# Where attention ends and the Fourier part begins in the branch stretch of the second block's two layers

## What is computed

```python
for l in range(DEPTH_2):                      # 2
    ...
    ux = hx @ w_in[l]
    uc = hc @ (w_in[l] if ctx_out else w_in[l][:, OFF_K:OFF_HQ])
    fx = fourier_mix(col(ux, OFF_FOURIER, FOURIER_W), w_four[l])
    ax, ac = attention_group(ux, uc, base_c, q_norm[l], k_norm[l], tabs, ctx_out)
    rx, rc = hgrn_group(ux, uc, base_c, lb_all[:, l], hg_norm[l], ctx_out)
    x = x + g_a * (jnp.concatenate([fx, ax, rx], axis=-1) @ w_out[l])
    x = x + g_f * swiglu(rmsnorm_2(x) * (1 + sc_f) + sh_f, w_gate[l], w_up[l], w_down[l])
    ...

def fourier_mix(u, w):                        # 4 groups of 64 features
    z = u.astype(jnp.float32).reshape(b, n, FOURIER_GROUPS, FOURIER_GD)
    z = jnp.fft.fftn(z, axes=(1, 3), norm="ortho").real
    return z.reshape(b, n, FOURIER_W).astype(u.dtype) @ w
```

## Time and profile before

| what | us |
| --- | --- |
| median of 3 runs | 2682.14 |
| lowest and highest of them | 2682.07 and 2695.03 |
| the profiled execution | 2682.28 |
| its span in the profile | 2680.5 |
| PE busy | 2499.0 (93%) |
| DVE, ACT, POOL busy | 874.3, 795.4, 784.0 |

### The profile page before, as it was taken

The page is one execution under the profiler, slowest core; times in us unless marked ns, Lnnn a source line. Parts: engine busy times, 40 slices in busy tenths (PEclk is TensorE's granted clock), DMA queues, the critical chain, the costliest instruction groups (busy, mean ns, idle before and its releaser), DMA issues.

```text
span 2680.5 us, 38133 instructions
## 1 busy us (share of the span) xinstructions
PE 2499.0 (93%) x16690; PEld 1926.0 (72%) x16690; DVE 874.3 (33%) x1301; ACT 795.4 (30%) x1016; POOL 784.0 (29%) x262
## 2 busy tenths in 40 slices
PE   7997888999999999979899999999799878899998
PEld 5884566777777786446788888888578336788886
DVE  3003236255257433832511111112451642311113
ACT  4222233223234423423322122122432433322222
POOL 2232143333333222502222222222221412344442
PEclk9997899999999999979999999999899878999999
DMA  4431023444443101002111111111211002222221
GB/s 171 166 140 32 17 95 142 172 157 157 157 169 139 57 9 46 3 2 95 48 63 63 63 63 59 68 41 62 73 40 46 2 2 95 79 95 95 104 93 55
DMA packets 41574, 216.70 MB, mean 81 GB/s; under 512 B 4088, under 2 KB 13064, under 8 KB 18112
## 3 DMA queue, kind: packets, MB, share of 16 engines
q1 hardware_dynamic: 37032, 206.55, 21.0%
q10 hardware_dynamic: 4376, 7.71, 0.9%
HBM read 212.12 MB, written 2.13 MB: 80 GB/s over the span
## 4 chain that ended last, share of the span: by engine, by line
PE 76%; DVE 7%; ACT 3%; issue 1%; POOL 0%; DMA 0%; DVEq 0%; ACTq 0%; POOLq 0%
PE PS L667 60%; PE PS L670 3%; PE PS L1087 2%; DVE s_states L1486 2%; PE PS L1120 2%; PE PS L744 1%; DVE a_lo L590 1%; PE PS L1683 1%; PE PS L1787 1%; DVE tmp L597 1%; PE PS L1882 1%; PE PS L1137 1%; PE PS L1099 1%; DVE x L610 1%; PE PS L728 0%
## 5 line engine op out<-in xcount | busy, mean ns | idle before, releaser
L2012 POOL TENSOR_TENSOR w_lo<-raw,w_hi 128x2048 fp32r<-128x2048 f32 (+2 forms) x146 | 650.8, 4457 | 1560.6 <-ACT w_hi L780 1560.6
L667 PE MATMUL PS<-a_hi,w_hi 128*128 128x512 f32 (+1 forms) x2104 | 702.4, 376 | 56.8 <-DVE a_lo L590 30.3
L667 PE MATMUL PS<-a_lo,w_hi 128*128 128x512 f32 (+1 forms) x2104 | 687.3, 369 | 0.0
L667 PE MATMUL PS<-a_hi,w_lo 128*128 128x512 f32 (+1 forms) x2104 | 681.9, 366 | 0.0
L667 PEld LDWEIGHTS PS<-a_hi,w_hi 128*128 128x128 f32 x2104 | 364.0, 191 | 154.6 <-issue 76.3
L667 PEld LDWEIGHTS PS<-a_hi,w_lo 128*128 128x128 f32 x2104 | 365.8, 192 | 68.9
L667 PEld LDWEIGHTS PS<-a_lo,w_hi 128*128 128x128 f32 x2104 | 365.3, 192 | 62.1 <-issue 0.7
L780 ACT ACTIVATE w_hi<-raw 128x2048 fp32r<-128x2048 f32 (+2 forms) x146 | 270.4, 1852 | 339.8 <-PE PS L667 185.1
L667 PE MATMUL PS<-hid_hi,w_hi 128*128 128x512 f32 (+1 forms) x784 | 260.5, 369 | 2.8 <-issue 2.8
L667 PE MATMUL PS<-hid_lo,w_hi 128*128 128x512 f32 (+1 forms) x784 | 260.9, 369 | 0.0
L667 PE MATMUL PS<-hid_hi,w_lo 128*128 128x512 f32 (+1 forms) x784 | 258.5, 366 | 0.0
(11 more groups left out here) (220 smaller groups left out, 2479.8 us busy)
## 6 DMA issues: line engine op xcount, KB each, us to landing
raw<-in_w_ada SPq DMA_DIRECT2D x48, 1024.0 KB, 6.9
raw<-in_w_ff SPq DMA_DIRECT2D x32, 1024.0 KB, 4.8
raw<-in_w_in SPq DMA_DIRECT2D x27, 1024.0 KB, 4.8
raw<-in_w_gate SPq DMA_DIRECT2D x22, 1024.0 KB, 4.8
raw<-in_w_up SPq DMA_DIRECT2D x22, 1024.0 KB, 4.8
raw<-in_w_down SPq DMA_DIRECT2D x16, 1024.0 KB, 4.7
raw<-in_w_out SPq DMA_DIRECT2D x12, 1024.0 KB, 5.5
raw<-in_w_down SPq DMA_DIRECT2D x8, 768.0 KB, 4.2
```

Of the source, the lines that this page charges most:

```text
L667: mm = p.matmul(ps[:, dst], wv[:, k, idx * P:(idx + 1) * P], av[:, k, dst], start=first, stop=last)
L2012: pool.tensor_tensor(w_lo[:, m % 2, 0:kt, 0:ncol], src, w_hi[:, m % 2, 0:kt, 0:ncol].bitcast(F32), ALU.subtract).then_inc(s_lo.sem, 1)
```

## The change

One constant. It is read by `att_pos`, through `other_pe`, `other_act` and `other_dve`, and by `four_pos`, so it moves attention and the Fourier part against the scan on PE, ACT and DVE, in both layers of the second block.

```diff
--- before.py
+++ after.py
@@ -1746,7 +1746,7 @@
                 except StopIteration:
                     left.remove(head)
 
-        ATT_SHARE = 0.8
+        ATT_SHARE = 0.7
         GATED_SHARE = 0.8
 
         def other_pe(p, l):
```

## The result

The changed kernel took 2715.07 us (median of four runs, 2708.99 to 2718.67), the kernel before 2683.72 beside it: 31 us or 1.2% between the medians, and a measured ratio of 1.0098, with an interval of 1.0079 to 1.0118. The forecast was 2676 with a range to 2688. The kernel became slower, by more than any of my cases gave.

What follows compares the result with a forecast made beforehand. TensorE, busy 93% of the span, was taken as the bound, with gains only in its idle or low-clock stretches. Layer 0's -2.9 and layer 1's -3.3 gave -6.2 us from 2682.28, so 2676.1; range 2667 to 2688.

Steps and rivals of the forecast that it cites:

- Covered edits: Readout and w_out panel behind the last outputs, VectorE's inverses: reordering there costs nothing; bounds 1.5 and 2 us.
- rival 4: The panel of w_out or an inverse is late by its bound: 2679 us, chance 0.1.
- Behind the last outputs: Feature tiles leave the stretch before the out projection: minus 4.5 us in layer 0, minus 5.0 in layer 1.
- From the third outputs' end to the last updates: Attention leaves this stretch, two tiles enter: minus 6.1 us in layer 0, minus 5.9 in layer 1.
- The last chain of states: VectorE's states before the last outputs: attention's product comes earlier, minus 0.4 us (layer 0) and 0.6 (layer 1); outputs still low-clocked.
- The same attention, earlier: Attention moved ahead hardly falls into waits: plus 5.1 us in layer 0, plus 6.7 in layer 1.
- net 0.8 worse: Layer 0's second scan half: a sum leaves, cover falls by 1.8 us, VectorE's chain then decides; net loss 0.8 us.
- Blocks: Scores move against instruction-block boundaries, changing stalls: plus 3.0 us in layer 0, 1.5 in layer 1; bounds minus 4 to plus 12.
- Rival 1: Three more block stalls than counted, in each layer's last two scores, plus low clock: +13, 2689 us, chance 0.12.
- Rival 2: Blocks come in time (-6.7 us), two tiles in the last wait keep the clock up: 2668 us, chance 0.13.
- Rival 3: It cancels: attention moved forward costs its length plus lost early-wait cover, as much as the end gains: 2682 us, chance 0.2.

Runs made afterwards that it cites:

- the root first: Changed kernel with ScalarE alone reordered, the readout's second root ahead of the second f_z: 2695.43 us, ratio to before 1.0032.
- with the outputs at full clock ahead of them: Kernel before, attention kept at 0.8, four feature tiles moved into the last wait, both roots ahead of the second f_z: 2674.64 us, ratio 0.9953.
- the shifted run: Changed kernel with the root first, plus 128 empty instructions on TensorE at the start of layer 0's stretch: 2707.00 us, about 2694 less these.
- the run that gives it back: Changed kernel with the root first, layer 0's second outputs one attention step and a sum later on TensorE: 2690.89 us, ratio 1.0007.
- at 0.77: Kernel before with the constant at 0.77, four Fourier tiles in the last wait, both roots ahead of the second f_z: 2692.40 us, ratio 1.0028.

## Why the prediction was wrong

*Covered edits: wrong, 17 to 20 us.* "Its split by ScalarE stands behind the second f_z anyway" was true and beside the point. I moved the means behind the first token transform and priced that, but did not see that ScalarE's list had turned over too: the second root now stood behind the second `f_z`, so that the panel's issue itself waited for the second transform. I gave it a bound of 1.5 us and rival 4 a chance of 0.1 with 2679; it was 7.0 to 9.3 per layer in the tails, and 17 to 20 us in the time.

*Behind the last outputs: right in layer 0 once the panel is in time, half right in layer 1.* Forecast -4.5 and -5.0. With the root first -3.7 and -2.8, and with the outputs at full clock ahead of them -5.4 and -4.9.

*From the third outputs' end to the last updates: near.* Forecast 12.4 us in layer 0, with two stalls; it was 13.7, with two. In layer 1 8.6 with a stall that did not come; it was 6.9.

*The last chain of states: right.* 9.0 to 8.7 us in layer 0 and 9.3 to 8.7 in layer 1, outputs at the low clock as expected.

*The same attention, earlier: wrong, and the largest miss.* I gave it +5.1 and +6.7 and the blocks +3.0 and +1.5. That is 8.1 and 8.2 us. The third outputs ended 23.5 us later in layer 0 (123.2 to 146.7) and 12.0 in layer 1 (122.5 to 134.5). The forecast's own 7.3 us of attention at full clock is in the 23.5. The stall at the first scores, at which I had put half of 2.2, cost 5.3 by the first outputs' end (the shifted run), and the second half's lost cover, "net 0.8 worse", was a wait of 3.02 us and cost 8.8 up to the third outputs' end (the run that gives it back). That is 21; these prices come from different runs and are not shown to add up. For the remaining 2 there is the second stall in the third scores (2.1 and slow work behind it), which no run took out alone, and chance: in five profiles of the order of before these outputs ended at 123.2 to 128.2 us. I saw both places. What failed is the price of the lost cover: I took 0.8 for a wait of 3.0 and put nothing for the work behind it, where the earlier trace rows had already shown the low clock behind a wait. For the blocks I did add low clock, but only half a stall at the first scores. Layer 1's excess of 3.8 stays open. Chance alone it is not, since these outputs ended at 118.8 to 122.5 us in five profiles of the order of before and at 131.0 to 134.9 in six of the new one.

*Blocks.* The stalls of layer 0 stood where I had counted them: one at the first scores, none over 1.1 us at the second, two each in the third and the last. Rival 1 was right in that a stall costs about twice its length or more (5.3 us for 2.4) and wrong in its place: the last scores had just what was counted. The shift by 128 instructions left the kernel before alone and gave 6 us to the new order, which then had three stalls in place of five.

*Rival 2* had "two tiles of real work in the hole" bring the clock back. Two did not (the last outputs took 6.8 us still). Four did where they reached up to the outputs, and did not in layer 0 at 0.77, with a wait of 3.70 us behind them. It rested on the earlier trace rows and on what the blocks cost. The Trainium skill ("Runtime: NRT & Kernel Launch", section "Instruction fetch mechanics") calls the cost of crossing a block mostly hidden; the trace does not agree, layer 0 of the changed kernel shows five stalls of 1.9 to 2.4 us.

*Rival 3* named the mechanism of the largest miss: attention that moves forward takes away cover in the early waits. It let that cost only as much as the end gains, 2682, with a chance of 0.2.

*Range and chances.* The top of the range, 2688, left out both causes: the late panel had a bound of 1.5 us, since I held the split's place for fixed, and the lost cover had no bound of its own, only the 0.8. Rival 1's 2689 came nearest the measured time, but by stalls in scores that had none too many.

## What to carry to other kernels

When two lists are laced by a fraction, don't price a shift by its size: count, for the old and the new value, how much work stands in each wait, and treat each wait that loses its cover as a new one, at its own length plus all that then runs at half the clock. Compare the order on every engine of the chain, not only on the one that is busy: a row that changes places with one that waits for another engine can hold up a transfer. And ask for the part of a change that does the good by itself; here it was four tiles in one wait, at its end, so that they ran right up to the work that had been slow.

## What the hardware showed that I had not expected

- A wait can cost TensorE more than its length: filling one of 3 us for the states made the stretch 7.3 to 8.5 us shorter. The Trainium skill ("TensorE: Matmul & The Clock Gate", section "HAM oscillation — how this bites in real kernels") tells of a kernel whose waits throw the engine back to 1.2 GHz again and again; the trace agrees, with outputs of 4.3 us that take 6.6 behind a wait of 3.0.
- VectorE's L1420 took 0.96 us alone and 2.03 beside POOL's sums, with the same operands. It looks like half the pace, but the single instructions take turns: L1420 began at 1128.17 us, the sum that ran then ended at 1129.38 and L1420 0.82 us behind it; the next sum began at 1129.46 and ended 1.12 us behind L1420, where a sum alone takes 1.27. The Trainium skill ("SBUF — State Buffer", section "Who interferes with whom") has a VectorE instruction with two inputs in SBUF contend with a GpSimd one that reads SBUF, and calls the contention an exclusive lock; the trace agrees.
- Waits that are long fulfilled are not free, some 0.1 us per instruction (13 us for 128, two waits counted as one instruction, at the start of a stretch), but 24 such instructions inside a running stretch left no idle time of over 1 us.
